# Attention pieces in twos on a ring of five banks, with three gate units moved to a later stage, in a three-block fp32 kernel

## The reference

```python
p = xn @ w_in                                  # 1024 x N_IN
p_tm = p[:, :SHIFT_COLS]                       # r, k, v and two low-rank parts
p_tm = p_tm + (previous_row(p_tm) - p_tm) * mu_shift
y_rwkv = rwkv7_time_mix(p_tm, p[:, RWKV_GATE0:ATT0], ...)      # ends in  * silu(gate)
y_att = mixed_dilated_attention(p[:, ATT0:ATT_GATE0], p[:, ATT_GATE0:])
h = h + concatenate([y_rwkv, y_att]) @ w_out
...
# mixed_dilated_attention: 16 heads of 64; patterns (window, dilation) = (128,1), (512,4), (2048,16)
s = einsum(q, k) / 8 in bands of 128 x 256;  m = max(s);  pexp = exp(s - m);  l = sum(pexp)
o = einsum(pexp, v) / l;   lse = m + log(l)
wts = softmax(lse over the three patterns);  return sum(wts * o) * silu(gate)
```

## Time and profile before

| | us |
|---|---|
| median of 3 runs | 3020.11 |
| the runs | 3020.28, 3012.93, 3020.11 |
| the profiled execution, its own time | 3013.84 |
| its span | 3012.5 |
| attention | 1094 to 1680 |
| the stage behind and the preparation | 1680 to 2092 |

### The profile page before, as it was taken

The page is one execution under the profiler, slowest core; times in us unless marked ns, Lnnn a source line. Parts: engine busy times, 40 slices in busy tenths (PEclk is TensorE's granted clock), DMA queues, the critical chain, the costliest instruction groups (busy, mean ns, idle before and its releaser), DMA issues. The chain is left out here.

```text
span 3012.5 us, 52417 instructions
## 1 busy us (share of the span) xinstructions
PE 2816.5 (93%) x21272; PEld 2196.6 (73%) x21272; DVE 1656.0 (55%) x3101; ACT 1270.5 (42%) x2322; POOL 221.9 (7%) x281
## 2 busy tenths in 40 slices
PE   8999999999997999999999999986887899989998
PEld 6766777776666777777777777765777778768776
DVE  3555755753366434555555466774556664552565
ACT  4343534332234435555556344432444334532234
POOL 0000000000000011111111003345400000000000
PEclk9999999999999999999999999997989999999999
DMA  3011111125234543333333325537524464421114
GB/s 117 29 42 34 38 56 32 55 69 180 79 98 140 162 127 79 86 86 86 86 86 87 94 98 160 157 120 292 158 92 151 143 217 133 154 82 43 36 64 153
DMA packets 188367, 316.57 MB, mean 105 GB/s; under 512 B 78288, under 2 KB 119520, under 8 KB 186464
## 3 DMA queue, kind: packets, MB, share of 16 engines
q1 hardware_dynamic: 188128, 313.23, 32.7%
HBM read 239.19 MB, written 73.99 MB: 104 GB/s over the span
## 5 line engine op out<-in xcount | busy, mean ns | idle before, releaser
L259 PE MATMUL ps<-xs,wparts 128*128 128x512 f32 (+1 forms) x1664 | 704.6, 423 | 11.7 <-DVE xs L1528 9.1
L261 PE MATMUL ps<-xs,wparts 128*128 128x512 f32 (+1 forms) x1664 | 657.3, 395 | 0.0
L260 PE MATMUL ps<-xs,wparts 128*128 128x512 f32 (+1 forms) x1664 | 655.6, 394 | 0.0
L327 DVE TENSOR_TENSOR wparts<-wring,wparts 128x1024 fp32r<-128x1024 f32 x248 | 305.5, 1232 | 320.9 <-ACT wparts L319 297.2
L259 PEld LDWEIGHTS ps<-xs,wparts 128*128 128x128 f32 (+1 forms) x1664 | 314.5, 189 | 135.4 <-issue 72.9
L319 ACT ACTIVATE wparts<-wring 128x1024 fp32r<-128x1024 f32 x248 | 262.8, 1060 | 287.3 <-PE ps L261 219.4
L261 PEld LDWEIGHTS ps<-xs,wparts 128*128 128x128 f32 (+1 forms) x1664 | 313.6, 188 | 72.9
L260 PEld LDWEIGHTS ps<-xs,wparts 128*128 128x128 f32 (+1 forms) x1664 | 315.1, 189 | 57.3 <-issue 3.3
L2524 DVE CUSTOM_DVE_ANT_0 Pm<-ps,mask 128x128 f32<-128x128 f32 (+1 forms) x384 | 111.0, 349 | 209.6 <-PE ps L2352 209.6
L2454 ACT ACTIVATE Pm<-Pm,ml 128x128 f32<-128x128 f32 (+1 forms) x384 | 168.2, 440 | 128.8 <-DVE ml L2524 128.6
L2301 POOL COPY perm<-qkg 128x1024 f32<-128x1024 f32 x32 | 63.3, 2011 | 1536.2 <-ACT qkg L363 1093.9
(11 more groups left out here) (410 smaller groups left out, 4816.7 us busy)
## 6 DMA issues: line engine op xcount, KB each, us to landing
wring<-in_wo SPq DMA_DIRECT2D x96, 512.0 KB, 3.5
ops<-rw SPq DMA_DIRECT2D x32, 640.0 KB, 6.2
wring<-in_w SPq DMA_DIRECT2D x39, 512.0 KB, 3.5
wring<-in_w2a SPq DMA_DIRECT2D x32, 512.0 KB, 6.3
wring<-in_w2u SPq DMA_DIRECT2D x25, 512.0 KB, 4.1
wring<-in_wg SPq DMA_DIRECT2D x24, 512.0 KB, 3.6
wring<-in_w2v SPq DMA_DIRECT2D x24, 512.0 KB, 4.2
MB<-wst SPq DMA_DIRECT2D x48, 256.0 KB, 4.9
```

The source lines that it names most:

```text
L259: nc.tensor.matmul(out, a, c, start=start, stop=False)
L260: nc.tensor.matmul(out, b, c, start=False, stop=False)
L261: return nc.tensor.matmul(out, a, d, start=False, stop=stop)
L327: K.nc.vector.tensor_tensor(W.part(i, 1), W.raw(i), W.part(i, 0).bitcast(F32), ALU.subtract).then_inc(*K.dve.done("w_lo", W.first + i))
```

## The change

1. In attention, pieces are taken in twos ("duos"), five to a pass. A duo has 7 steps, a pass 35. Step 0 has the values of both pieces of duo g - 2 and then the scores of both of duo g; the four following steps have one half-piece's turns each, of duo g - 1. The chain of duos runs over the borders of the passes, and its last two duos are drained (`main(K, B, 8)`) together with the tail of pair 7 and the stage behind. The maximum and the exponential are ordered and signalled by half-pieces, on a `Pm` of six shelves (before: three slots of two).
2. Scores, turns, `w_t` and one group of values share one ring of five banks (RS); the other values have one bank (RO). The stage behind has two banks for its units (before: four).
3. The RWKV gates of the pairs 5, 6 and 7 become units of the preparation (`GATED`). Attention has 29 units (before: 32): three in the passes 0 to 2 (paced 2 of 3), four in the passes 3 to 6 (11 of 12), three filling units in pass 7 as before. The preparation's passes 5, 6 and 7 have 3, 3 and 2 units (before: 2, 2 and 1). Their gates are stored by `gate_out`, three more places on SP's queue.
4. On SP, `values_load(p, 2)` and `rg_store` move to the next pass, behind its first `w_load`.

```diff
-    return 1 + 3 * p + x
-BEHIND, PASSES, LAST_AT = [(0, 0), (0, 1), (0, 2), (1, 0)], [3] * 5 + [2, 2, 1], 17
+    return 1 + 3 * p + x if x < 3 else 25 + p - GATED[0]
+BEHIND, PASSES, LAST_AT = [(0, 0), (0, 1), (0, 2), (1, 0)], [3] * 7 + [2], 17
+GATED = (5, 6, 7)
...
+            if at == first[p] + 3 and p == 7:
+                yield from gate_out(K, A, B, 5)
...
+    yield from gate_out(K, A, B, 6)
     yield from rwkv_first_sp(K, A, B.rw)
     yield from prep_store(K, A, B, NP - 1)
+    yield from gate_out(K, A, B, 7)
...
+def gate_out(K, A, B, p):
+    K.sp.wait_ge(*(yield "uev", PREP_W0 + prep_unit(p, 3), 1))
+    K.nc.sync.dma_start(A["rw"][p][:, 6144:7168], B.spare[:, 1, :]).then_inc(*K.sp.done("rg_store", p, slot="_late", by=16))
...
-    B.RU = at.RU.join(at.RS)
+    B.RU = at.RU
...
-    B.RM = at.RT.join(at.RO)
+    B.RU, B.RM = at.RU.join(at.RS.part([0, 1])), at.RS.part([2, 3, 4]).join(at.RO)
...
+    if x == 3:
+        yield from unit_act(K, B.W, prep_unit(p, 3), B.spare[:, 1, :], ACT.Silu,
+                            before=[("rg_store", p - 1)] if p > GATED[0] else [])
+        return
...
-    return 4 * p + x + (2 if p < 7 else 0)
+        return x + (att_first(p - 1) if p else 0)
+    s = p + SHIFT if x == 3 else p
+    return att_first(s) + x - (0 if s < 7 else 2)
+SHIFT = 3
+def att_first(s):
+    return 2 + 3 * s + max(0, s - SHIFT)
...
+ND2 = NS // 2
+def duo(g):
+    return divmod(g, ND2) if 0 <= g < 8 * ND2 else None
+def side(g, j):
+    (p, d), (x, h) = duo(g), divmod(j, 2)
+    return p, 2 * d + x, h
+def shelf(B, g, j):
+    return B.Pm[:, (4 * g + j) % 6, :]
+def duos(p):
+    return range(ND2 * p, ND2 * p + (ND2 if p < 8 else 2))
...
-        for i in range(4 * p + 4, 4 * p + 8):
+        for i in range(att_first(p) + 2, att_first(p + 1) + 2):
             if p < 7:
                 yield from w_load(K, B.W, i)
-            if p and i == 4 * p + 4:
-                yield from rg_store(K, A, B, p - 1)
-                yield from weights_move(K, A, B, p - 1)
+            if i == att_first(p) + 2:
+                if p > SHIFT:
+                    yield from rg_store(K, A, B, p - 1 - SHIFT)
+                if p:
+                    yield from values_load(K, A, B, p, 2)
+                    yield from weights_move(K, A, B, p - 1)
         if p == 7:
             yield from prep_early_sp(K, A, B.prep)
         if p < 7:
@@ -2207,17 +2255,16 @@
         if p:
             yield from att_store(K, A, B, p - 1)
         yield from stats_move(K, A, B, p)
-        for pi in (1, 2):
-            if p < 7:
-                yield from values_load(K, A, B, p + 1, pi)
+        if p < 7:
+            yield from values_load(K, A, B, p + 1, 1)
...
+def scores_pe(K, B, p, i):
+    nc, pe, s = K.nc, K.pe, PIECES[i]
+    qk = [B.qkg[:, p % 2, x, :] if s.pi == 0 else B.perm[:, s.pi - 1, x, :] for x in range(2)]
+    banks = [B.RS.take(("a_s", p, i, h), ("a_max", p, i, h)) for h in range(2)]
...
+def values_pe(K, B, p, n):
+    nc, pe, s = K.nc, K.pe, PIECES[n]
+    if s.first:
+        ring = B.RS if (s.pi, s.gg) == (2, 1) else B.RO
+        _, old = ring.take(("a_o", p, s.pi, s.gg), ("a_osc", p, s.pi, s.gg))
...
+def turn_pe(K, B, g, j):
+    nc, pe, (p, n, h) = K.nc, K.pe, side(g, j)
+    bank, old = B.RS.take(("a_t", p, n, h), ("a_pt", p, n, h))
+    pe.wait_ge(*(yield "a_exp", p, n, h))
+    if old:
+        pe.wait_ge(*(yield old))
+    for x, b in enumerate(PIECES[n].blocks):
+        a = nc.tensor.transpose(bank[:, half(x, 128)], shelf(B, g, j)[:, b[0]:b[0] + 128], K.ident)
+    a.then_inc(*pe.done("a_t", p, n, h))
...
+    for g in duos(p):
+        for x in range(2):
+            if duo(g - 2):
+                yield from values_pe(K, B, *side(g - 2, 2 * x)[:2])
+        for x in range(2):
+            if duo(g):
+                yield from scores_pe(K, B, *side(g, 2 * x)[:2])
+        yield STEP
+        for j in range(4):
+            if duo(g - 1):
+                yield from turn_pe(K, B, g - 1, j)
+            yield STEP
...
-    for _ in range(TURN + 4):
-        yield STEP
-    bank, old = B.RT.take(("w_t", p), ("w_row", p))
+    for _ in range(TURN + 5):
+        yield STEP
+    bank, old = B.RS.take(("w_t", p), ("w_row", p))
...
-                         paced(units(K, B, p + 1), 6, 7) if p < 7 else paced(fill(K, B), 2, 3))
-    yield from weave(tail(K, B, 7), behind(K, B.prep, 0))
+                         paced(units(K, B, p + 1), *((11, 12) if p >= SHIFT else (2, 3))) if p < 7 else paced(fill(K, B), 2, 3))
+    yield from weave(main(K, B, 8), tail(K, B, 7), behind(K, B.prep, 0))
...
-    B.RS, B.RT, B.RO = rows.part([0, 1]), rows.part([2, 3]), rows.part([4, 5])
+    B.RS, B.RO = rows.part([0, 1, 2, 3, 4]), rows.part([5])
...
+def max_dve(K, B, g, j):
...
+    if 4 * g + j >= 6:
+        dve.wait_ge(*(yield ("a_t", *side(*divmod(4 * g + j - 6, 4)))))
...
+def turn_dve(K, B, g, j):
+    nc, dve, (p, n, h) = K.nc, K.dve, side(g, j)
+    w = 128 * len(PIECES[n].blocks)
+    if duo(g - 1):
+        dve.wait_ge(*(yield ("a_av", *side(g - 1, j)[:2])))
+    dve.wait_ge(*(yield "a_t", p, n, h))
+    nc.vector.tensor_copy(B.PT[:, n % 2, h, 0:w], K.bank["a_t", p, n, h][:, 0:w]).then_inc(*dve.done("a_pt", p, n, h))
...
+    for g in duos(p):
+        for j in range(5):
+            if j < 4 and duo(g):
+                yield from max_dve(K, B, g, j)
+            if j and duo(g - 1):
+                yield from turn_dve(K, B, g - 1, j - 1)
+            yield STEP
+        for _ in range(2):
+            yield STEP
```

More of the change, by code:

```diff
@@ L1994, in prep_unit_dve @@
     yield from w_lo(K, B.W, prep_unit(p, x) + 1)
+    if x == 3:
+        for _ in range(5):
+            yield STEP
+        return
     for _ in range(4):
@@ new lines, in scores_pe @@
+def scores_pe(K, B, p, i):
+    nc, pe, s = K.nc, K.pe, PIECES[i]
+    qk = [B.qkg[:, p % 2, x, :] if s.pi == 0 else B.perm[:, s.pi - 1, x, :] for x in range(2)]
+    banks = [B.RS.take(("a_s", p, i, h), ("a_max", p, i, h)) for h in range(2)]
+    if s.pi == 0:
+        pe.wait_ge(*(yield "uev", ATT_W0 + att_unit(p, 1), 1))
+    else:
+        pe.wait_ge(*(yield "perm", p, s.pi))
+    for _, old in banks:
+        if old:
+            pe.wait_ge(*(yield old))
+    for c, two, lo, hi in s.cells:
+        for rr, (bank, _) in zip(RH, banks):
+            a = nc.tensor.matmul(bank[:, lo:hi], qk[0][rr, half(c, 128)],
+                                 qk[1][rr, 128 * (c - 1) if two else 128 * c:128 * c + 128], start=True, stop=True)
+    a.then_inc(*pe.done("a_s", p, i))
@@ new lines, in values_pe @@
+def values_pe(K, B, p, n):
[3 more added lines that the diff above has]
+        _, old = ring.take(("a_o", p, s.pi, s.gg), ("a_osc", p, s.pi, s.gg))
+        if old:
+            pe.wait_ge(*(yield old))
+    ob = K.bank["a_o", p, s.pi, s.gg]
+    pe.wait_ge(*(yield "a_pt", p, n, 1))
+    pe.wait_ge(*(yield "vc", p, s.pi))
+    for x, (lo, c, kc, new, end) in enumerate(s.blocks):
+        for h, rr in enumerate(RH):
+            a = nc.tensor.matmul(ob[rr, half(c % 4, 128)], B.Vc[:, 8 * s.pi + kc, rr], B.PT[:, n % 2, h, half(x, 128)],
+                                 start=new, stop=end, skip_group_check=True)
+    a.then_inc(*pe.done("a_av", p, n))
@@ new lines, in exp_act @@
+def exp_act(K, B, g, j):
+    nc, act, (p, n, h) = K.nc, K.act, side(g, j)
+    s, ml, P = PIECES[n], B.ml2[:, p % 2], shelf(B, g, j)
+    if p >= 2:
+        act.wait_ge(*(yield "w_mul", p - 2))
+    act.wait_ge(*(yield "a_max", p, n, h))
+    for c, two, lo, hi in s.cells:
+        a = nc.scalar.activation(P[:, lo:hi], P[:, lo:hi], ACT.Exp, scale=-1.0, bias=ml[:, s.pi, c, h, 0:1],
+                                 accum_out=ml[:, s.pi, c, h, 1:2])
+    a.then_inc(*act.done("a_exp", p, n, h))
@@ new lines, in out_act @@
+def out_act(K, B, p, s):
+    nc, act = K.nc, K.act
+    d, n = group(B.O2[:, p % 2, s.pi, :], s.pi, s.gg)
+    act.wait_ge(*(yield "a_av", p, PIECES.index(s)))
+    if p >= 2:
+        act.wait_ge(*(yield "att_store", p - 2))
+    act.in_order()
+    nc.scalar.activation(d, runs(K.bank["a_o", p, s.pi, s.gg], n), ACT.Copy).then_inc(
+        *act.done("a_osc", p, s.pi, s.gg))
+def att_act_main(K, B, p):
+    for g in duos(p):
+        for x in range(2):
+            if duo(g - 2):
+                q, n, _ = side(g - 2, 2 * x)
+                if PIECES[n].last:
+                    yield from out_act(K, B, q, PIECES[n])
+        yield STEP
+        for j in range(4):
+            if duo(g):
+                yield from exp_act(K, B, g, j)
+            yield STEP
+        for _ in range(2):
+            yield STEP
@@ L2477, in att_act_tail @@
     nc.scalar.activation(B.w3[:, :, :, :], B.w3[:, :, :, :], ACT.Exp).then_inc(*act.done("w_exp", p))
-    for _ in range(4):
+    for _ in range(5):
         yield STEP
```

156 lines of the change are left out of this document (37 added, 119 removed).

## The result

The changed kernel took a median of 2997.71 us in five runs (2991.8 to 3003.38), the kernel before 3014.66 (3012.93 to 3020.28, five runs). The ratio is 0.9937, its 95% interval 0.9922 to 0.9951: 17 to 19 us faster, clear of noise. The forecast, 2983, was 15 us too low, though its range (2968 to 3006) holds the result. The forecast of the gain, 32.9 us, is twice the 17.0 between the medians; the point sat on a base of 2983 + 32.9 = 3015.9, 1 us above the median of all five runs of before.

What follows compares the result with a forecast made beforehand. PE bounds attention; the preparation is mixed, with DMA engines full at its end. Terms -33.0 - 25.6 + 7.0 + 3.7 + 2.7 + 12.3 = -32.9 us give 2980.9 or 2987.2 by base; point 2983, range 2968 to 3006.

Steps and rivals of the forecast that it cites:

- rival (b): Preparation passes 5 to 7: moved units are paid in full, +33 instead of +12.3, giving 3004 us; chance 0.10.
- Three units leave attention: Attention: 48 matmuls a unit at 0.229 us, 11.0 us each, all saved on PE; -33.0 us.
- Grouping: Attention: joined blocks of values and scores save the edges between kinds of matmuls on PE; -25.6 us.
- Rival (a): Attention: grouping buys nothing, edges move to halved turns or the ring gives it back; about 3009 us, chance 0.12.
- Stage behind: Stage behind attention: with two unit banks instead of four, units wait for the token shift; +7.0 us.
- Pass 7: Attention pass 7: a turn waits for a maximum behind late `w_lo`, +3.7 us, and the clock falls, +2.7.
- Preparation's end: Preparation passes 5, 6 and 7: one more unit each, partly on idle PE, and one more gate store; +12.3 us.
- "Covered at nothing": POOL: Attention: POOL's 7.93 us per pass was taken as covered, costing nothing.
- Rival (c): Stage behind and pass 7: their stalls are hidden, without 13.4 us of cost; 2970 us, chance 0.15.
- Rival (d): Attention duos: the ring of five locks PE to DVE; at 1.5 us per duo 3042 us, chance 0.06.
- the two stalls: Waits in the stage behind and in pass 7, forecast at 7.0 + 3.7 + 2.7 us.

Runs made afterwards that it cites:

- move_only: The kernel before with only the three gate units moved from attention to the preparation, pieces and rings as before; 2996.98 us, ratio 0.9938 to before.
- perm_late: The changed kernel with POOL's copies for the third pattern waiting for the pass's last maximum; 2985.83 us, ratio 0.9902 to before.
- group_clean: Duos and ring of five with all 32 units in attention, plus later POOL copies, earlier weight load and two more unit banks behind; 2988.41 us, ratio 0.9903 to before.
- split: The changed kernel with later POOL copies, earlier load, two more unit banks, and a duo's values one step ahead of the next duo's scores; 2978.11 us.
- four_banks: The changed kernel with the stage behind taking two of the ring's five banks to its own two; 2989.32 us, ratio 0.9906 to before.
- load_ahead: The changed kernel with the preparation's first w_load ahead of weights_move(6) on SP in attention pass 7; 2988.25 us, ratio 0.9912 to before.
- again: The changed kernel executed once more, unedited; 3000.01 us, ratio 0.9954 to before.

## Why the prediction was right, and where it was off

The direction and the terms that the sum has were right; POOL's part was left out, and the gain came out at half of the forecast. That the range holds the result is in part luck: the lower gain has a cause that no rival names. The own range of the forecast, 2970 to 2998, just holds 2997.71 and does not hold the second median, 3000.01; the rest, up to 3006, was opened for rival (b), which did not come. Term by term, as the prediction has them:

- **Three units leave attention, -33.0.** Measured 3 x 12.1 = 36 in move_only and 3 x (70.86 - 59.25) = 35 in perm_late. The term priced 48 matmuls at 0.229. In the order on PE, a pass of three units also has fewer separate blocks between unit matmuls (23 instead of 25 in move_only, 20 instead of 25 in perm_late), so edges go with the unit; how much of the 1.1 us a pass they are was not measured apart.
- **Grouping, -25.6.** Measured 26.4 by marks and 28.3 by medians (group_clean). The edge of 0.20 is confirmed by split (0.19). Halved turns cost nothing: four take 0.36 us where eight took 0.79. Rival (a) is refuted: group_clean has the same matmuls as the kernel before. With it falls, for this kernel, a distance that goes by the number of columns alone, as the Trainium skill has it for the isolated gap ("TensorE: Matmul & The Clock Gate", section "Back-to-back issue gap").
- **Stage behind, +7.0.** Of 9.1 us of waits four_banks takes away 8.4 and brings 1.5 back in front of L1868: 6.9. By marks up to the end of the preparation's first pass, with that return, it is 7.6 against the first profile of the changed kernel and 9.9 against the second. Right in mechanism and nearly in size.
- **Pass 7, +6.4.** Its cause, the load behind `weights_move(6)`, is shown by load_ahead, worth 7.0 to 8.5. The step that failed is who waits: I followed the queue behind `w_lo` on DVE (a wait of 4.9 was forecast) and not the one behind `w_hi` on ACT, where a group's eviction holds the only bank of RO (6.7 measured).
- **Preparation's end, +12.3.** The marks give 12.1 (again) to 14.3: the passes 5 and 6 took 44.3 to 45.5 and 44.3, and RWKV began 62.6 and 63.5 after the start of pass 7 instead of 58.8. The full price of rival (b), 33, is refuted.
- **"Covered at nothing": POOL.** This was the error. It checked POOL's busy share (7.93 us a pass) and not when its copies run, though the trace of before already has a product of 2.26 beside them. The collision costs 12.3 to 12.6 us in the passes 0 to 6 and 12 to 14 of median.

With the measured terms, rounded: -35 - 26.4 + 12.3 + 9 + 8 + 13 is -19. The marks from the first scores to the start of RWKV give -18.8 in both profiles (998.0 before; 979.2 and 979.2), the medians -17.0 and -15.0. The forecast's -33 lacks 12 to 13 for POOL and 4 for the two stalls; longer units and grouping give 3 back. The base of 3015.9 took 1 us off the distance between point and result. Rival (c), that the stalls are hidden, was wrong for this kernel; load_ahead and four_banks show what they cost. Rival (d), a lock between DVE and PE in each duo, did not come: waits for the maximum in a pass of four units are 0.9 us in all.

## What to carry to other kernels

Where an order is packed tighter, ask of every engine that is far from busy not how much it does but beside whom it now does it: two operations that follow the same block of matmuls can start together, and where VectorE's had two inputs in SBUF and GpSimd copied there, one waited for the other. Follow a late load on each engine that has an instruction for it, to the first thing queued behind that holds a bank. And compare stages by marks in the profile before comparing medians, since a stage at a changing clock, 9 us apart in two executions of one kernel here, can hide a gain or make one up.

## What the runs showed of the hardware

- Two VectorE operations of 1.23 us each took 3.00 and 2.75 beside two GpSimd copies, and the copies 1.96 and 2.90; moved apart the operations took 1.22 and 1.23.
- A block of scores or values between matmuls of 128x512 cost PE 0.19 to 0.20 us for both edges (0.32 to 0.34 instead of 0.23 from start to start). A block of turns showed an edge only behind it (0.31), and four turns took 0.36 to the next start where eight took 0.79, so halving them cost 0.01 us or less.
- The same RWKV stage, over the profiles here, took between 440.2 us at a granted clock of 0.95 and 453.1 at 0.91, with equal work on the other engines.
